# Banded attention: F32R operand triples replaced by plain float32 products with column halves, and its first steps placed inside the last input-projection tile

## The reference, cut to what matters

```
z = rmsnorm(x) @ w_in                              # 2816 columns: 22 tiles of 128
a_val, a_gate, q, k, v, g_b, g_c, h_c = split(z)
y_a = silu(layernorm(causal_dwconv(a_val*sigmoid(a_gate), width 31) + b))
q, k = rmsnorm per head (8 heads of 64)
s = q k^T / 8 + bias[clip(i - j)]     # query block of 128 sees up to 5 key tiles of 128
o = softmax(s) v
y = [rmsnorm(y_a), rmsnorm(o), rmsnorm(y_c)] @ w_out
```

## Time and profile before

| | |
|---|---|
| median of 3 runs | 1658.76 us |
| profiled execution | 1654.98 us |
| its span, first to last instruction | 1653.2 us |
| mean granted TensorE clock | 0.985 of full speed |
| PE busy | 1580.5 us, 96% |
| DVE busy | 966.6 us, 58% |
| ACT busy | 639.4 us, 39% |
| POOL busy | 276.7 us, 17% |
| DMA | 189.35 MB, mean 115 GB/s |

### The profile page before, as it was taken

One profiled execution on the slowest core, in us unless ns is written; L12 is line 12 of the kernel. 1 busy time (PEld: TensorE's weight loads), 2 busy tenths in 40 slices (PEclk: granted clock), 3 DMA queues, 4 the chain that ended last, 5 costly groups with the idle time before them and its releaser, 6 DMA issues.

```text
span 1653.2 us, 27261 instructions
## 1 busy us (share of the span) xinstructions
PE 1580.5 (96%) x11100; PEld 1530.2 (93%) x11100; DVE 966.6 (58%) x1389; ACT 639.4 (39%) x1138; POOL 276.7 (17%) x342
## 2 busy tenths in 40 slices
PE   6999999997889999998989999999999989999999
PEld 6999999996878899997669999999999989999999
DVE  6625776536778744233643486666666548656653
ACT  5521021126889522113432263333333424333332
POOL 1011000002220010000000006444444411010110
PEclk9999999988999999999999999999999999999999
DMA  7424111002110153302131215344343786354563
GB/s 242 148 91 164 49 39 39 26 1 94 37 37 34 40 173 141 107 14 77 43 92 68 79 42 188 141 146 147 146 146 148 251 291 209 96 167 146 162 211 112
DMA packets 63665, 189.35 MB, mean 115 GB/s; under 512 B 7872, under 2 KB 13048, under 8 KB 63408
## 3 DMA queue, kind: packets, MB, share of 16 engines
q1 hardware_dynamic: 37904, 91.11, 17.4%
q0 software_dynamic: 25648, 96.65, 16.4%
HBM read 138.58 MB, written 54.12 MB: 117 GB/s over the span
## 4 chain that ended last, share of the span: by engine, by line
PE 83%; DVE 5%; DMA 4%; ACT 4%; issue 2%; POOL 1%; SPq 0%; ACTq 0%; DVEq 0%; POOLq 0%
PE ps L429 33%; PE ps L2640 18%; PE ps L2661 17%; PE ps L2170 3%; PE ps L458 3%; PE ps L2418 2%; PE ps L2538 2%; DMA a<-wdn 2%; PE ps L2506 1%; PE ps L2358 1%; PE ps L2396 1%; DVE scores L1740 1%; ACT scores L1191 1%; PE ps L480 1%; DVE t_raw L2019 1%
## 5 line engine op out<-in xcount | busy, mean ns | idle before, releaser
L429 PE MATMUL ps<-A_hi,w_hi 128*128 128x364 f32 x768 | 172.9, 333 | 0.0
L429 PE MATMUL ps<-A_lo,w_hi 128*128 128x364 f32 x768 | 169.7, 329 | 0.0
L429 PE MATMUL ps<-A_hi,w_lo 128*128 128x364 f32 x768 | 169.5, 329 | 0.0
L383 DVE TENSOR_TENSOR w_lo<-w_raw,w_hi 128x1024 fp32r<-128x1024 f32 x43 | 52.4, 1223 | 148.2 <-ACT w_hi L379 147.7
L379 ACT ACTIVATE w_hi<-w_raw 128x1024 fp32r<-128x1024 f32 x42 | 44.2, 1057 | 239.6 <-PE ps L429 136.2
L429 PEld LDWEIGHTS ps<-A_lo,w_hi 128*128 128x128 f32 x768 | 134.1, 189 | 0.0
L429 PEld LDWEIGHTS ps<-A_hi,w_lo 128*128 128x128 f32 x768 | 133.7, 188 | 0.0
L429 PEld LDWEIGHTS ps<-A_hi,w_hi 128*128 128x128 f32 x768 | 133.1, 189 | 0.0
L2640 PE MATMUL ps<-t_hi,wq_hi 128*128 128x272 f32 x480 | 99.5, 288 | 5.3 <-issue 2.9
L2661 PE MATMUL ps<-r_hi_a,wq_hi 128*128 128x272 f32 x448 | 93.5, 290 | 7.0 <-DVE r_lo_a L2105 6.5
L2640 PE MATMUL ps<-t_lo,wq_hi 128*128 128x272 f32 x480 | 99.2, 288 | 0.0
(11 more groups left out here) (328 smaller groups left out, 3954.1 us busy)
## 6 DMA issues: line engine op xcount, KB each, us to landing
w_raw<-slabs SPq DMA_DIRECT2D x68, 512.0 KB, 3.8
quads_d<-quad_sum POOLq DMA_DIRECT2D x64, 272.0 KB, 2.9
w_raw<-wdn POOLq DMA_DIRECT2D x32, 512.0 KB, 4.2
r_raw_a<-quads_d SPq DMA_DIRECT2D x56, 272.0 KB, 3.1
r_raw_b<-quads_d SPq DMA_DIRECT2D x56, 272.0 KB, 2.9
quads_d<-hid_stage POOLq DMA_DIRECT2D x48, 272.0 KB, 3.0
Y<-xT POOLq DMA_DIRECT2D x16, 546.0 KB, 4.7
y_d<-Y POOLq DMA_DIRECT2D x16, 546.0 KB, 3.1
```

The costliest lines, as they stand in the source:

```text
L383: e.tensor_tensor(WL[:, par], RAW[:, par], WH[:, par].bitcast(F32), ALU.subtract).then_inc(s.w_lo, 1)
L429: ins = e.matmul(PS[:, 3 * par + c, 0:CH], wt[:, wpar, w], xt[:, col:col + CH], start=(first and n == 0 and m == 0), stop=(last and n == l ...
```

## The change

Nothing outside the mixer is touched. In the attention:

- Splits are gone. q, k, the cached keys and values, v and the probabilities are used as plain float32: q_hi, k_hi, qk_lo, cache_hi, cache_lo, v_hi are removed, v_lo becomes v_copy (DVE, one copy), the cache DMAs write straight to KC and VC.
- Scores: one plain product for each column range and head.
- Values: for each key tile one plain product for each head, with that head's 64 columns of v and 128 moving columns, into that head's 64 partitions of bank 7. o_out is one copy for both heads.
- Of each unit's transposed pieces ACT copies piece 0 and DVE the others.
- PE does values(n-1) ahead of items_a(n).

At the start:

- Tile 21 is cut: k steps 0 to 3, items (0,0) and (0,3), k 4 and 5, the statistic of ya, scores(0), k 6 and 7, then scores(1) and items (0,1), (0,4), (0,6). The other four items of the first pair go into units 0 and 1, and items 6 to 8 of the second pair into units 3, 5 and 6.
- The reciprocal of the head statistics, and the two copies that spread it, run before tile 20's result is used (i == 20 instead of 21).
- The first bias load waits for the last convolution tap and the state outputs instead of ya_done and tile 21, and stands ahead of the v outputs in POOL's queue. Buffers are placed anew so that its tile is free by then.
- Four small memsets move from before the loop to unit 4.

```diff
@@ tensor engine
+            e.wait_ge(s.w_lo, S_OUT)
+            e.wait_ge(s.tile_read, S_OUT - 2)
+            pe_part(e, 1, 1, A, range(4), last=False)
+            item(0, 0)
+            item(0, 3)
+            pe_part(e, 1, 1, A, (4, 5), first=False, last=False)
+            e.wait_ge(s.g_sum, 3)
+            e.wait_ge(s.k_nrm, 1)
+            pe_stat(e, cnt, (TT[:, :],), ONE, N_PE_BC)
+            n_rc += 1
+            e.wait_ge(s.tile_read, S_OUT - 1)
+            scores(0)
+            pe_part(e, 1, 1, A, (6, 7), first=False)
+            scores(1)
+            for x in FIRST_ITEMS[2:]:
+                if x == 4:
+                    e.wait_ge(s.stat_read, cnt.stat)
                 item(0, x)
             e.wait_ge(s.tile_read, S_OUT)
-            scores(0)
-            scores(1)
             for n in range(N_U):
                 transposes(n)
+                if n:
+                    values(n - 1)
                 for j, x in items_a(n):
                     item(j, x)
-                if n:
-                    values(n - 1)
                 if n + 2 < N_U:
                     scores(n + 2)
...
+                def part(h, op):
+                    keys_, k, w, c = op
                     rows = slice(64 * h, 64 * h + 64)
-                    return e.matmul(score_cols(n, h)[0][:, c:c + w], r.Q[qx][rows, q0:q0 + P], K[kx][rows, k:k + w],
-                                    start=(m == 0), stop=(m == 2))
+                    return e.matmul(score_cols(n, h)[0][:, c:c + w], Q[rows, q0:q0 + P], keys_[rows, k:k + w],
+                                    start=True, stop=True)
...
+                part(0, X[0]).then_inc(s.s_done, 1)
+                part(1, M[1])
                 if b == 8:
+                    part(1, (K, SEQ, 64, 512))
+                part(0, M[0]).then_inc(s.s_done, 1)
+                e.wait_ge(s.s_done, S_CUM[n] + 1)
+                part(1, X[1]).then_inc(s.s_done, 1)
...
+                    for h in range(2):
+                        rows = slice(64 * h, 64 * h + 64)
+                        ins = e.matmul(PS[rows, 7, 0:P], lhs[:, rows], rhs[:, h * P:(h + 1) * P],
+                                       start=(kt == 0), stop=(kt == tiles - 1))
@@ gpsimd
+                elif j == 0:
+                    g.wait_ge(s.conv_step, 64)
+                    g.wait_ge(s.state_out, 96)
...
+            g.wait_ge(s.rep_out, 16)
+            load_bias(0)
             g.wait_ge(s.tile_read, S_IN + 22)
@@ scalar
+            def pt_copy(n):
+                rows, w = piece(n, 0)
+                e.wait_ge(s.t_done, CUM[n] + 1)
+                if n >= 2:
+                    e.wait_ge(s.pv_done, 2 * (n - 1))
+                e.activation(pt_piece(n, 0), PS[0:rows, 4, 0:w], ACT.Copy).then_inc(s.pt_act, 1)
@@ vector
+            def pt_copy(n):
+                for p in range(1, pieces(n)):
                     rows, w = piece(n, p)
+                    e.wait_ge(s.t_done, CUM[n] + p + 1)
+                    if n >= 2:
+                        e.wait_ge(s.pv_done, 2 * (n - 1))
+                    e.tensor_copy(pt_piece(n, p), PS[0:rows, 4 + p, 0:w]).then_inc(s.pt_dve, 1)
...
+            e.wait_ge(s.ya_done, 2)
+            item(0, 0)
+            item(0, 3)
+            group_sum(2)
+            biased(0)
+            evac(21, QKV[11][:, :])
+            biased(1)
+            dve_recip(e, cnt)
+            for x in FIRST_ITEMS[2:]:
                 item(0, x)
```

More of the change, by code:

```diff
@@ L131, in __init__ @@
         self.k_nrm = sem("k_nrm")
[L132 to L137, removed]
+        self.v_copy = sem("v_copy")
         self.s_done = sem("s_done")
@@ L290, in build @@
             AT.append(BandOperands(
[L291 to L304, removed]
+                V=at(f"v{r}", [P, 9, P], F32, o + 4 * TB),
+                KC=at(f"kc{r}", [P, 512], F32, o + 4 * TB + 9216),
+                VC=at(f"vc{r}", [P, 4, P], F32, o + 4 * TB + 13312)))
+        SS = [[at(f"scores{r}{h}", [P, 640], F32, B0 + o) for h, o in enumerate(offs)]
+              for r, offs in enumerate(((9488, 12048), (14608, 0)))]
+        BIAS = [at("bias0", [P, 2, 640], F32, B0 + TB), at("bias1", [P, 2, 640], F32, W0 + 18432)]
+        PT = [at(f"pt{r}", [P, 4, 256], F32, W0 + 5120 * r) for r in range(2)]
+        PT5 = [at(f"pt5{r}", [P, 256], F32, W0 + 5120 * r + 4096) for r in range(2)]
         RX = at("rstd_heads", [P, 9, 2, 64], F32, R0)
-        RX0 = at("rstd_heads_q0", [P, 9, 2, 64], F32, B0 + 4128)
+        RX0 = [at(f"rstd_heads_{n}0", [P, 9, 2, 64], F32, Y0 + 3 * TB + o) for n, o in (("q", 0), ("k", 4608))]
         ESUM = at("exp_sums", [P, 36, 2], F32, c1 + 192)
         EREC = at("exp_recs", [P, 36, 2], F32, c1 + 192 + 288)
-        RKC = at("kc_raw", [P, 512], F32, R0 + 4608)
-        RVC = at("vc_raw", [P, 4, P], F32, R0 + 6656)
         BX = at("bias_ext", [8, 768], F32, B0 + 5 * TB)
@@ L575, in score_cols @@
             return PS[:, 0:3].rearrange("p a b -> p (a b)")[:, c0:c0 + cols], c0
+        S_CUM = [0]
+        for n in range(N_U):
+            S_CUM.append(S_CUM[-1] + (3 if n % 9 >= 4 else 2))
         RXN = {(0, 0): 1, (0, 1): 2}
@@ L1069, in _, with group_sq @@
             sigmoid(1)
-            def group_sq(tiles, ready, cnt_ready):
+            def group_sq(tiles, ready, cnt_ready, other):
                 e.wait_ge(ready, cnt_ready)
@@ L1173, in prepare @@
                     rstd_heads(j, 0)
-                if i == 2:
-                    cache_hi(j)
                 if i == 3:
                     rstd_heads(j, 1)
-                if i == 4:
-                    q_hi(j)
-                if i == 5:
-                    k_hi(j)
-                for _, x in items_b(n):
-                    if x >= 6:
-                        v_hi(j, x - 6)
             def exps(n):
@@ L1229, in _ @@
             cnt.bc += N_ITEM + 3
-            rstd_heads(0, 1)
-            q_hi(0)
-            k_hi(0)
-            for c in range(3):
-                v_hi(0, c)
             exps(0)
             for n in range(N_U):
-                pt_hi(n)
+                pt_copy(n)
                 if n + 1 < N_U:
@@ L1811, in _ @@
                     biased(n + 2)
-                if n == 1:
-                    cache_lo(e, 0)
                 for j, x in items_b(n):
                     item(j, x)
+                if n == 4:
+                    e.wait_ge(s.bc_done, N_DVE_BC + ITEM[0, 5])
+                    for i in range(2, 6):
+                        e.memset(y(i)[:, TOK:T], 0.0).then_inc(s.pad_ready, 1)
                 if n == 29:
@@ L2253, in _ @@
             n_rc = 1
-            for i in range(3, 22):
+            for i in range(3, 21):
                 win_tile(i)
@@ L2411, in values @@
                     w = min(P, cols - kt * P)
-                    for m, (vx, px) in enumerate(((0, 0), (0, 1), (1, 0))):
-                        if b < 8:
-                            lhs = r.V[vx][:, max(0, b - 4) + kt]
-                        else:
-                            lhs = r.VC[vx][:, kt] if kt < 4 else r.V[vx][0:w, 8]
-                        rhs = PT[n % 2][px][0:w, kt] if kt < 4 else PT5[n % 2][px][0:w, :]
-                        ins = e.matmul(PS[:, 7, 0:256], lhs, rhs,
-                                       start=(kt == 0 and m == 0), stop=(kt == tiles - 1 and m == 2))
```

263 lines of the change are left out of this document (95 added, 168 removed).

## The result

| | before | after | forecast |
|---|---|---|---|
| median, us (4 runs each) | 1658.20 | 1619.31 | 1630 |
| lowest to highest | 1654.12 to 1661.41 | 1617.70 to 1620.73 | range 1617 to 1652 |
| profiled execution / its span | 1654.98 / 1653.2 | 1619.95 / 1617.8 | 1626.0 |
| PE / DVE / ACT / POOL busy | 1580.5 / 966.6 / 639.4 / 276.7 | 1569.3 / 943.7 / 590.0 / 252.3 | |

After over before is 0.9766 (95% interval 0.9742 to 0.979): faster. The median lies inside the range, but only 2.3 us above its lower end. The two profiled spans differ by 35.4 us, the medians by 38.9, since the profiled execution of before lay 3.2 under its median and that of after 0.6 over. The profile explains the 35.4.

The account below looks back on a forecast made before the run. It took TensorE as the bound, 83% of the chain of waits. Opening -8.6, first pair -5.3, middle pairs -9.6, last pair -5.5 sum to -29.0 us: 1658.8 - 29 = 1630, range 1617 to 1652 (8 in 10).

Parts of the forecast that it names:

- values as cover: Attention loop: PE's values before item_a give 1.4 us of cover; waits of 0.97, 0.69 and 0.75 go, 1.62 shrinks.
- A: The forecast itself: row and column halves both overlap in the attention; 1620 to 1637 us with bounds on stalls; chance 0.60.
- The price of plain float32: Attention products: a plain product costs near 4 column passes where the F32R triple costs 3; slower by a third like for like.
- A middle pair: Second and third head pair of the attention loop: 34.5 us each against 39.3, -4.8, twice.
- Scores: Attention scores: four plain matmuls in overlapping row halves, 1.2 us a full unit; 9.5 us a head pair, now 10.0.
- Values: Attention value products: column halves overlap, 0.213 us a key tile; 10.2 us a head pair, now 12.8.
- Items: Broadcasts and transposes on PE in the attention loop: 12 a head pair at 0.37 us, 4.4 before and after.
- Stalls: PE's waits in a head pair: from 4.2 us to 2.6, bounds 0.5 and 4.2, left for short units.
- The first pair: First head pair of the attention loop: 35.4 us, with +0.9 for extra items, against 40.7; -5.3.
- The last pair: Last head pair: no head items, but ScalarE's other work stalls PE; 34.0 us against 39.5, -5.5.
- The opening: From tile 21 to the first probability transpose: it comes at 383.9 us instead of 392.57, -8.6.
- late bias: First bias load in the opening: left behind tile 21, ready near 392 us, and the opening would save nothing.

Follow-up runs that it names:

- x1: Changed kernel with column halves undone: each key tile one plain product with all 128 columns of v and 256 moving columns; 1640.23 us, ratio 0.9907 to before.
- y1: Kernel before with only PE's values(n-1) put ahead of items_a(n); 1647.37 us, ratio 0.9939 to before.
- x6: Changed kernel with PE's items_a put back ahead of values(n-1); 1629.29 us, ratio 0.9833 to before.
- x2: Changed kernel with both heads' value products in the same column half, partitions 0 to 63; 1647.57 us, ratio 0.995 to before.
- z1: Changed kernel with PE's items_a ahead of values(n-1), and items_b ahead of biased(n+2) on VectorE; 1615.75 us, ratio 0.9763 to before.
- x4: Changed kernel with tile 21's eight k steps in one piece, items, statistic and first scores behind it; 1626.13 us, ratio 0.9821 to before.
- x7: Changed kernel with ScalarE copying all pieces of the transposed probabilities, VectorE none; 1621.3 us, ratio 0.9782 to before.
- x5: Changed kernel with the first bias load waiting again for ya_done and tile 21, its new queue place kept; 1624.83 us, ratio 0.9808 to before.
- x3: Changed kernel with values of head 0 over all key tiles first, then those of head 1; 1640.49 us, ratio 0.9904 to before.
- x8: Changed kernel with scores of 5-key-tile units issued head by head instead of alternating; 1620.13 us, ratio 0.9784 to before.

## Why the prediction was right, and where it was off

The forecast was 29.0 us; the same stretches measured 35.8. The mechanism, halves that overlap and values as cover, is the one that the runs show, but the sum fell short. Its own bounds for A ended at 1620, just above the measured 1619.31. By its own steps:

- **The price of plain float32** held. A plain matmul is two records, 0.216 a record of 256 columns in x1, as in the earlier trace rows; and x1 against y1 shows it dearer than a triple at full width.
- **A middle pair**, by PE's kinds of work, each counted from its start to the start of the next kind, so that a change of kind counts with what stands ahead of it:

| us a pair | before | after | forecast: before | forecast: after |
|---|---|---|---|---|
| transposes | 8.38 | 8.70 | 7.8 | 7.8 |
| values | 13.64 | 9.30 | 12.8 | 10.2 |
| scores | 9.17 | 9.44 | 10.0 | 9.5 |
| items | 3.84 | 5.24 | 4.4 | 4.4 |
| idle | 4.21 | 0.45 | 4.2 | 2.6 |
| sum | 39.24 | 33.13 | 39.2 | 34.5 |

The same rows in the runs (here the idle time counts every gap):

| us a middle pair | y1 | x6 | x1 | x2 | z1 |
|---|---|---|---|---|---|
| transposes | 7.35 | 8.70 | 7.86 | 8.70 | 8.22 |
| values | 13.32 | 9.22 | 15.16 | 16.73 | 9.32 |
| scores | 9.21 | 9.43 | 9.72 | 9.43 | 9.43 |
| items | 5.10 | 5.09 | 4.99 | 5.26 | 4.94 |
| idle | 1.54 | 3.37 | 0.02 | 0.00 | 0.36 |

- **Scores**: 9.44 as forecast. What they took before was put 0.8 too high (9.17 instead of 10.0), so they gain nothing and lose 0.3.
- **Values**: the mechanism held, taken from row halves by likeness and shown by x1 and x2. They gain more than forecast, 4.3 instead of 2.6, partly a matter of booking: transposes and values together are 18.0 in after both ways.
- **Items** were mis-sized: they cost 1.4 more than before, forecast nothing. In before most stand between transposes and values, all of the whole array. The new order alone puts them next to scores (y1, 5.10), the halves alone put them next to values in halves (x6, 5.09), and each brings the same cost. Part is booking: in y1 the transposes fall by 1.0 as the items rise, and its four busy rows come to what before's do, 35.0. So the order costs PE no work there, and its gain is idle time. Over these four busy rows the change is -2.35 (35.03 to 32.68), forecast -3.1: the changes of kind that the halves add were priced in the values alone.
- **Stalls** are the term that failed: forecast 4.2 to 2.6, measured 4.21 to 0.45, more than the whole difference between -4.8 and -6.1. The forecast moved the values as cover and then still kept more than half of the waits, for short units in which scores, bias, exp and transposes follow each other. Those didn't wait: the two rows of waits above are all, and both are items. Even the lower bound of 0.5 was above what came, 0.45. The gain in stalls was put some 2.1 too low and that in the busy rows some 0.8 too high, so the pair as a whole came out closer than its terms. x6 has 3.29 idle, and x6 and y1 price the order at 2.7 to 2.8 a pair.
- **The first pair**: -7.3 against -5.3, 33.40 us where the forecast had 35.4. Of the 2.0, 1.4 is what the middle pairs missed by too. The rest is most of the 0.9 for its extra items. They do cost more than that (items 6.54 instead of 5.24), but from first transpose to first transpose this pair holds the values of 8 units only, 7.97 instead of 9.30, and that takes it back. The low clock of before is part of the gain, not of the miss, since it was in the measured 40.7: its transposes and scores take 2.4 more there than in a middle pair. That the clock would stay up in after was taken for granted; x4 shows 1.2 lost where it doesn't.
- **The last pair**: 34.0 against 32.06. The forecast left PE stalled by ACT's other work. x7 shows that such a stall exists if ACT does all the copies: 2.0 us more, and PE's idle time is 2.2 instead of 0.7. This is the one place where the relief of ACT from copies is shown to count.
- **The opening** held to 0.1: 383.9 and 383.89. x4 and x5 show both parts needed, the interleaving for 3.5 and the early bias for 7.3 us. The two are more than the 8.8 gained in all, so they share a part: without the early bias 1.5 us of gain is left, without the interleaving 5.3. The step that a late bias would be ready "near 392" and the opening would save nothing isn't tested as it stands, since x5 kept the new place: there it was ready 21.9 us after the start of tile 21, which is 387 on the prediction's count.
- **The rest of the gap** to 1630, near 4 of 10.7 us, is no mechanism: the profiled execution of before was 3.2 under its median and that of after 0.6 over.

Not tried: column halves with F32R triples. Whether they would beat the plain ones, with fewer passes but with the splits kept, stays open. The scores, whose halves overlap in both kernels, warn against giving the credit to plain float32: with triples they took 9.17 a pair, plain 9.44. What the runs show is that halves pay, not that plain products do. Also open is what sets the reach of the look-ahead, three records in x3 and in x8.

## What to carry to other kernels

When two independent products each fill only half the columns (or half the rows) of the array, put them in different halves and alternate them in the program; here that made plain float32 values cheaper than full-width triples, though one by one they are dearer. Count the changes between full-width products and halves as well, 0.1 us each, and put small full-width work next to full-width work. Ask of each wait of the bound engine whether another call of the same engine can stand ahead of it: swapping two calls gave 2.8 us of the 6.2 a pair, with no arithmetic changed. When work is pulled into a tile, pull its transfers too, and count openings from a common event rather than from the start of the program. Before you put a miss down to something in the old kernel, ask whether the forecast had already started from the measured value.

## What the runs showed of the hardware

- Column halves of plain float32 run side by side: ten products of 128 columns in 1.24 us in two halves (after), 2.32 in one half (x2).
- PE starts a matmul of the other half ahead of earlier ones in the program, but only over three records, one and a half plain matmuls: x8 lost nothing (33.18 against 33.13), x3 4.7 us a pair.
- A record of a plain matmul took the same for each moving column with 64 or 128 columns of weights: 0.109 us for 128 (x2), 0.216 for 256 (x1).
- A change between products of the whole array and products in halves cost 0.1 us (0.11 by z1 against after).
- In x4, PE busy 3.26 of 6 us was followed by 6 us at a mean granted clock of 0.55, so mostly at 1.2 GHz; in before the low clock lasted over most of 384 to 402. Work then took twice as long, beside the wait itself: scores(1) 1.27 us instead of 0.63.
